# A three-block transformer kernel: other waits at the start and in its norms, masks on POOL, MLP features half by half

## The reference, cut to what matters

```python
for layer in range(2):
    hn = rmsnorm(h, mix_norm[layer])
    h = h + (moba_nsa_mixer(hn, ...) if layer % 2 == 0 else fox_mixer(hn, ...))
    h = h + sqrelu_mlp(rmsnorm(h, mlp_norm[layer]), mlp_w1[layer], mlp_w2[layer])
x = rmsnorm(h, final_norm)
# second_block: shifts, scales and gates sh1 ... gt3 come from silu(c) @ w_ada + b_ada
n = modulate(rmsnorm_2(x, g_ffn1), sh1, sc1); h = x + 0.5 * gt1 * swiglu(n, ...)
n = modulate(rmsnorm_2(h, g_mix), sh2, sc2);  h = h + gt2 * hybrid_mixer(n, ...)
n = modulate(rmsnorm_2(h, g_ffn2), sh3, sc3); h = h + 0.5 * gt3 * swiglu(n, ...)
return rmsnorm_2(h, g_final)
# in fox_mixer: s = q k / 8 + cum[query] - cum[key], masked where key > query, then softmax
```

## Time and profile before

| | us |
|---|---|
| median of 3 runs | 1121.64 |
| lowest and highest | 1120.15, 1125.65 |
| the profiled execution, its own time | 1123.69 |
| its span, first to last instruction | 1121.9 |
| PE busy in the span | 1086.5 (97%) |
| DVE busy | 783.7 (70%) |
| ACT busy | 648.2 (58%) |
| POOL busy | 98.6 (9%) |

### The profile page before, as it was taken

The page is one execution under the profiler, slowest core; times in us unless marked ns, Lnnn a source line. Parts: engine busy times, 40 slices in busy tenths (PEclk is TensorE's granted clock), DMA queues, the critical chain, the costliest instruction groups (busy, mean ns, idle before and its releaser), DMA issues.

```text
span 1121.9 us, 15908 instructions
## 1 busy us (share of the span) xinstructions
PE 1086.5 (97%) x6118; PEld 922.1 (82%) x6118; DVE 783.7 (70%) x1275; ACT 648.2 (58%) x1048; POOL 98.6 (9%) x195
## 2 busy tenths in 40 slices
PE   6999999999999999999999999999989999999997
PEld 5888878888887997888888778888878978888885
DVE  6567767777777666776766768887875766665565
ACT  6656766555566776664645664444455767444443
POOL 1022210010000121100000001101000110000000
PEclk9999999999999999999999999999999999999999
DMA  7742248888855633677778547777644434555551
GB/s 301 289 155 83 102 141 308 292 292 297 295 201 183 246 130 114 235 268 248 266 259 313 193 143 289 264 295 288 220 153 150 152 117 154 190 190 187 189 190 60
DMA packets 39515, 236.71 MB, mean 211 GB/s; under 512 B 4453, under 2 KB 4613, under 8 KB 16528
## 3 DMA queue, kind: packets, MB, share of 16 engines
q1 hardware_dynamic: 26640, 188.76, 46.9%
q0 software_dynamic: 12512, 46.26, 11.6%
q10 hardware_dynamic: 288, 0.68, 0.2%
HBM read 234.58 MB, written 1.10 MB: 210 GB/s over the span
## 4 chain that ended last, share of the span: by engine, by line
PE 84%; DVE 7%; ACT 5%; issue 2%; DMA 2%; SPq 0%; DVEq 0%; ACTq 0%
PE bank L1451 21%; PE bank L1420 15%; PE bank L1422 14%; PE bank L1421 14%; PE bank L1452 11%; PE bank L1625 2%; DMA raw<-in_stream 2%; DVE w_lo L981 1%; ACT w_hi L631 1%; PE bank L1607 1%; DVE w_lo L970 1%; PE bank L1596 1%; PE bank L1519 1%; ACT w_hi L620 1%; PE bank L1595 1%
## 5 line engine op out<-in xcount | busy, mean ns | idle before, releaser
L1451 PE MATMUL bank<-a_two,w_hi 128*128 128x512 f32 x1088 | 386.3, 398 | 0.0
L981 DVE TENSOR_TENSOR w_lo<-raw,w_hi 128x2048 fp32r<-128x2048 f32 x123 | 278.5, 2289 | 109.1 <-ACT w_hi L631 109.1
L1452 PE MATMUL bank<-a_two,w_lo 128*128 128x256 f32 x1088 | 305.2, 281 | 0.0
L631 ACT ACTIVATE w_hi<-raw 128x2048 fp32r<-128x2048 f32 x123 | 232.1, 1909 | 49.7 <-DMA raw<-in_stream 49.7
L1451 PEld LDWEIGHTS bank<-a_two,w_hi 128*128 128x128 f32 x1088 | 204.4, 188 | 49.6
L1452 PEld LDWEIGHTS bank<-a_two,w_lo 128*128 128x128 f32 x1088 | 205.4, 189 | 1.7
L1420 PE MATMUL bank<-w_lo,hid_hi 128*128 128x512 f32 x432 | 169.6, 393 | 3.6 <-DVE w_lo L981 2.4
L1421 PE MATMUL bank<-w_hi,hid_lo 128*128 128x512 f32 x432 | 168.5, 390 | 0.0
L1422 PE MATMUL bank<-w_hi,hid_hi 128*128 128x512 f32 x432 | 168.5, 390 | 0.0
L797 ACT ACTIVATE cross<-bank 128x256 f32<-128x256 f32 x136 | 44.8, 382 | 203.7 <-PE bank L1452 203.7
L970 DVE TENSOR_TENSOR w_lo<-raw,w_hi 128x1024 fp32r<-128x1024 f32 x102 | 124.5, 1238 | 31.3 <-ACT w_hi L620 30.5
(11 more groups left out here) (212 smaller groups left out, 1489.2 us busy)
## 6 DMA issues: line engine op xcount, KB each, us to landing
raw<-in_stream SPq DMA_DIRECT2D x173, 1024.0 KB, 5.0
ada_raw<-in_ada POOLq DMA_DIRECT2D x72, 512.0 KB, 5.2
cmpw<-in_stream SPq DMA_DIRECT2D x4, 1024.0 KB, 8.4
rel_band<-rel_scratch POOLq DMA_DIRECT2D x2, 1024.0 KB, 10.9
cum_row<-cum_scratch POOLq DMA_DIRECT2D x4, 512.0 KB, 7.2
h<-in_x SPq DMA_DIRECT2D x2, 512.0 KB, 6.5
raw<-in_stream SPq DMA_DIRECT2D x2, 512.0 KB, 7.6
silu_row<-in_c_row POOLq DMA_DIRECT2D x2, 512.0 KB, 4.6
```

Source lines behind the costliest of these rows:

```text
L631: nc.scalar.activation(w_hi[:, u % RING, :], raw[:, u % RING, :], ACT.Copy).then_inc(hi_ready, 2)
L981: nc.vector.tensor_tensor(w_lo[:, u % RING, :], raw[:, u % RING, :], w_hi[:, u % RING, :].bitcast(F32), ALU.subtract).then_inc(lo_ready, 2)
L1451: nc.tensor.matmul(ps[bank][:, 0:2 * T], wh[:, k, cols_], a_two[:, :, k, :], start=k == 0, stop=False)
L1452: ins = nc.tensor.matmul(ps[bank][:, T:2 * T], wl[:, k, cols_], a_hi[:, k, :], start=False, stop=k == KT - 1)
```

## The change

**Start.** DVE zeroes part of `probT` first, and PE runs `WARM` = 30 products on these zeros. PE no longer waits for `rpick` before it turns tile 0; tile 1 is turned after two value parts instead of three, and parts of unit 0 come before unit 1. ACT and DVE take the turned chunks one at a time (`split_no` numbers them), with the weights' halves between; two chunks share a bank (`turned_at`). The large second piece of `par` goes from ACT's queue, first of all, to SP's behind unit 3.

**First mixer.** `nq0` uses bank 7 instead of 4, so the wait for `pairs_taken` moves to `qm0`; `compress` of the second kind waits for bank 7; the turn of `hid30` moves from (`nq1`, 3) to (`qm0`, 0), and what hangs on it one tick later.

**Fox mixer.** The mask product on PE is gone. POOL adds the triangle to the key part of the bias, into `cum_early` (tile 0) and in place (tile 1).

**Norms.** The mean of the first half is taken while the second is squared, ACT's root adds the second sum as its bias, one Newton operation goes. ACT scales both tiles, in pieces of 256, 256 and 512 columns, and squares tile 1 between the chunks of tile 0. DVE makes the inverse root of tile 1 before the second weight half. `two_inverse_roots` is cut in `two_means`, `both_norms_root` and `first_norm_root`.

**MLPs.** Chunk 0 of a feature unit gets all eight contraction tiles, then chunk 1; `rests` takes chunk 0 when `half_done` says so. POOL begins the modulation's transfers only after the third unit of the MLP, `silu_row` is made after F3, and the columns begin with j = 3. **End.** The output goes out in quarters, half of them from ACT's queue.

The core of the diff:

```diff
+WARM = 30
+        cum_early = place("cum_early", [P, 16, P], at=V_at + 2 * D * 4)
         def fox_bias(hh, t):
-            return cum_row[:, hh, 0:(2 * P if t else P)]
+            return cum_row[:, hh, :] if t else cum_early[:, hh, :]
-        STACKS = {("kskw", 0): (5, True, 4), ("nq0", 0): (4, False, 4), ("nq1", 0): (5, False, 6),
+        STACKS = {("kskw", 0): (5, True, 4), ("nq0", 0): (7, False, 4), ("nq1", 0): (5, False, 6),
-            ... {"mlp0": (2, FF1 - 2), "mlp1": (2, FF1 - 4), "glu0": (1, FF2 - 3)}[name]
+            ... {"mlp0": (3, FF1 - 3), "mlp1": (3, FF1 - 5), "glu0": (1, FF2 - 3)}[name]
...
 # POOL
+            def mask(c):
+                pool.wait_ge(cum_landed[c], 16)
+                four = slice(4 * c, 4 * c + 4)
+                tri = pc_("tri", P).unsqueeze(1).to_broadcast([P, 4, P])
+                pool.tensor_tensor(cum_early[:, four, :], cum_row[:, four, 0:P], tri, ALU.add).then_inc(masked, 1)
+                pool.tensor_tensor(cum_row[:, four, P:T], cum_row[:, four, P:T], tri, ALU.add).then_inc(masked, 1)
+            pool.wait_ge(unit_used, FIRST["mlp0"] + 3)
             silu_input()
             modulation_weights(*ADA_OF["mlp0"])
...
 # ACT
             def root(name, t):
                 act.wait_ge(mean_ready, 2 * NORMS.index(name) + t + 1)
                 if name != "gf1":
-                    nc.scalar.activation(stat[:, 3, t:t + 1], stat[:, 2, t:t + 1], ACT.Sqrt).then_inc(root_ready, 1)
+                    act.wait_ge(sumsq, squares_before(name, t) + 2)
+                    nc.scalar.activation(stat[:, 3, t:t + 1], stat[:, 1, t:t + 1], ACT.Sqrt, bias=stat[:, 2, t:t + 1]).then_inc(root_ready, 1)
+            def scale(name, t):
+                act.wait_ge(inv_ready, NORM[name] + t + 1)
+                inv = fin[:, t, 12:13] if name == "gf1" else stat[:, 7, t:t + 1]
+                for c0, c1 in ((0, 256), (256, 512), (512, 1024)):
+                    nc.scalar.activation(tok[:, t, c0:c1], h[:, t, c0:c1], ACT.Copy, scale=inv).then_inc(rows_scaled_act, 1)
             def norm_turn(name, gain, shift=None):
-                for t in range(TT):
-                    squares(name, t)
-                    ...
+                squares(name, 0)
+                round_half()
+                scale(name, 0)
+                turned(name, 0, gain, shift, (0, 1))
+                square_half(name, 1, 0)
+                turned(name, 0, gain, shift, (2, 3))
+                square_half(name, 1, 1)
+                round_half()
+                root(name, 1)
+                scale(name, 1)
+                turned(name, 1, gain, shift)
             def mlp(name):
                 begin(name)
-                silu_of_c(1 if name == "mlp0" else 2)
...
+                        rests(0, MLP_BANKS[j % 2], crossed, HALF_BEFORE[name] + j - 1, u0 + n + 1)
+                        if j == 3:
+                            silu_of_c(1 if name == "mlp0" else 2)
...
 # DVE
             def norm_turn(name, sums, gain, shift=None, gate=None):
...
-                rest_half()
                 if fused:
                     weigh(1, 0)
+                    two_means(1)
                     weigh(1, 1)
-                    two_inverse_roots(1)
+                    both_norms_root(1)
                 else:
                     inverse_root(name, 1)
-                scale(name, 1)
+                rest_half()
                 turned(name, 1, gain, shift)
...
 # PE
             def wide_unit(u, banks):
-                for half in range(2):
-                    for nt in range(2):
-                        wide_part(u, banks[nt], nt, (half,))
+                for nt in range(2):
+                    wide_part(u, banks[nt], nt)
-                if kind == "fox":
-                    ins = nc.tensor.matmul(bank[:, P:3 * P], ident_r[:, :], tri_r[:, :].unsqueeze(1).to_broadcast([P, 2, P]),
-                                           start=False, stop=True)
+            for _n in range(WARM):
+                nc.tensor.matmul(ps[0][:, 0:P], probT[:, 0, 0:P], probT[:, 0, 0:P], start=True, stop=True)
-                    if tag == "nq0" and part == 0:
+                    if tag == "qm0" and part == 0:
                         pe.wait_ge(pairs_taken, 2)
```

More of the change, by code:

```diff
@@ L480, in build @@
         CROSS_BEFORE = {"mlp0": -4, "mlp1": 2 * FF1 - 8, "glu0": 4 * FF1 - 10, "glu1": 4 * FF1 + 2 * FF2 - 12}
+        HALF_BEFORE = {"mlp0": 0, "mlp1": FF1 - 2, "glu0": 2 * FF1 - 4, "glu1": 2 * FF1 + 2 * FF2 - 6}
         BEGIN = {"mlp0": 0, "mlp1": 1, "glu0": 2, "glu1": 3}
@@ L493, in ada_pieces @@
                 return range(0)
-            (first, last), j0, n = ADA_OF[name], *{"mlp0": (2, FF1 - 2), "mlp1": (2, FF1 - 4), "glu0": (1, FF2 - 3)}[name]
+            (first, last), j0, n = ADA_OF[name], *{"mlp0": (3, FF1 - 3), "mlp1": (3, FF1 - 5), "glu0": (1, FF2 - 3)}[name]
+            if j < j0:
+                return range(0)
             return range(first + (last - first) * min(j - j0, n) // n, first + (last - first) * min(j - j0 + 1, n) // n)
@@ L873, in even_extras @@
                         nc.scalar.activation(hid_e[:, v, :], ps[(2, 7)[v]][HD:HD + 30, 0:256], ACT.Copy).then_inc(hidden_half, 1)
-                for v, where in enumerate((("qm0", 0, 0), ("km0", 0, 2))):
+                for v, where in enumerate((("qm0", 0, 1), ("km0", 0, 2))):
                     if tick.at(*where):
@@ L950, in _ @@
                 act.wait_ge(inv_ready, NORM["last"] + t + 1)
-                nc.scalar.activation(tok[:, t, 0:512], ada_raw[:, t, 0:512], ACT.Copy, scale=stat[:, 7, t:t + 1]).then_inc(out_ready_act, 1)
+                for k in range(2):
+                    quarter = slice(256 * k, 256 * k + 256)
+                    nc.scalar.activation(tok[:, t, quarter], ada_raw[:, t, quarter], ACT.Copy, scale=stat[:, 7, t:t + 1]).then_inc(out_ready_act, 1)
+                for k in range(2):
+                    quarter = slice(256 * k, 256 * k + 256)
+                    act.wait_ge(out_ready_act, 2 * t + k + 1)
+                    act.dma_start(out[t * P:(t + 1) * P, quarter], tok[:, t, quarter]).then_inc(out_stored, 16)
         @block.vector
@@ new lines, in polish, with both_norms_root @@
+            def polish(t, v, root, y, b):
+                f = fin[:, t, :]
+                chain(nc.vector.reciprocal(f[:, y:y + 1], f[:, root:root + 1]))
+                chain(nc.vector.scalar_tensor_tensor(out=f[:, b:b + 1], in0=f[:, v:v + 1], scalar=f[:, y:y + 1], in1=f[:, y:y + 1],
+                                                     op0=ALU.mult, op1=ALU.mult))
+            def both_norms_root(t):
+                f = fin[:, t, :]
+                dve.wait_ge(mean_ready, NORM["gf1"] + t + 1)
@@ L1309, in even_extras @@
                                                 e, ALU.mult).then_inc(hidc_ready, 1)
[L1310 removed]
+                if tick.at("qm0", 0, 3):
                     dve.wait_ge(kc_hi, 1)
@@ L1403, in scale_out @@
             def scale_out(t):
-                half = slice(512, D)
-                nc.vector.scalar_tensor_tensor(out=tok[:, t, half], in0=h[:, t, half], scalar=stat[:, 7, t:t + 1], in1=row[:, half],
-                                               op0=ALU.mult, op1=ALU.mult).then_inc(out_ready, 1)
+                for k in range(2):
+                    quarter = slice(512 + 256 * k, 768 + 256 * k)
+                    nc.vector.scalar_tensor_tensor(out=tok[:, t, quarter], in0=h[:, t, quarter], scalar=stat[:, 7, t:t + 1], in1=row[:, quarter],
+                                                   op0=ALU.mult, op1=ALU.mult).then_inc(out_ready, 1)
             for t in range(TT):
@@ L1447, in wide_part @@
                 cols_ = slice(nt * P, nt * P + P)
-                for half in halves:
+                for half in range(2):
                     wait_weights(u, half)
@@ L1704, in even_extras @@
                         compress(c // 2, c % 2)
-                for v, where in enumerate((("nq1", 0, 3), ("km0", 0, 1))):
+                for v, where in enumerate((("qm0", 0, 0), ("km0", 0, 1))):
                     if tick.at(*where):
```

259 lines of the change are left out of this document (150 added, 109 removed).

## The result

The changed kernel takes 1112.37 us (median of 7 runs, 1111.13 to 1115.68) against 1120.87 us (7 runs, 1119.64 to 1125.65): a ratio of 0.9921, 95% interval 0.9910 to 0.9932, some 8.5 us faster. The time lies inside the predicted range, 4.6 us above the predicted value. Its profiled execution took 1113.3 us for a span of 1111.5, so the two profiled spans differ by 10.4 us.

What follows compares the result with a forecast made beforehand. The prediction took PE, busy nearly the whole span, as the bound. Its terms, -8.0 (start and first mixer), -0.7, -1.7, -2.35, -0.6 and -0.5, sum to -13.85, taking 1121.64 to 1107.8 us; range 1101.5 to 1114.5.

Steps and rivals of the forecast that it cites:

- masks of 2 us and more: Fox mixer: sign of a wrong prediction, which took POOL's masks at 1.2 us each.
- feature units of `glu0` that wait for weights: MLPs: sign of a wrong prediction, which took 0 for the weights of all 68 feature units.
- Start, -3.8 taken: Start: first value product 1.2 and 0.4 us earlier, 2.6 from the clock, less 0.4 for waits.
- The clock's 2.6 us: Start: 5.5 us of value products at the low level would run at the high one, about 2.6 us less.
- 30 take 4 us at the high level and twice that, 8, at the low: Start: the thirty products on zeros would be hidden, or late by a few tenths of a us.
- Rival A: Start: the clock is low when the values begin, taking back 2.6 us, 1110.4; chance 0.16.
- First mixer, -4.2 taken: First mixer: the pairs' wait goes, 1.8 us, the low clock behind it, 1.5, and the `hid30` wait, 0.9.
- `nq0` no longer waits for the pairs: -1.8: First mixer: the wait, moved to `qm0`, goes because ACT takes the pairs long before; 1.8 us.
- Rival B: First mixer: transfers bound it, half of start and mixer's gain, 4 us, is lost, 1111.8; chance 0.14.
- Fox, -0.7 taken: Fox mixer: sixteen mask products saved on PE, -2.7 us, against a new wait for POOL taken as 2.0.
- Rival C: Fox mixer: POOL's masks run slowly beside DVE, adding 9.5 us or more, 1117.3 to 1118.8; chance 0.09.
- Norms, -2.35 taken: Norms: shorter waits for scaled tiles, 0.85 us in `gf1`, 1.2 in `gmix` and `gf2`, 0.1 each in three others.

Runs made afterwards that it cites:

- e2: The changed kernel with 20 products on zeros instead of 30; 1115.12 us, ratio 0.9948.
- e3: The changed kernel with the wait for the pairs put back ahead of `nq0`; 1112.63 us, ratio 0.9928.
- e12: The changed kernel with the pairs' wait back ahead of `nq0` and unit 4 loaded only when unit 1 is used up; 1115.53 us, ratio 0.9943.
- e6: The changed kernel with `silu_row` and POOL's modulation transfers back at the beginning of `mlp0` and `mlp1`; 1115.89 us, ratio 0.9948.
- e7: The changed kernel with only POOL's modulation transfers begun at once in `mlp0` and `mlp1`, `silu_row` still after F3; 1113.40 us, ratio 0.9926.
- e10: The changed kernel with the old order in the feature units, half then chunk; 1114.97 us, ratio 0.9937.
- e4: The changed kernel with POOL's masks of pieces 2 and 3 behind the first and third head's scaling; 1112.37 us, ratio 0.9923.
- e11: The changed kernel with twenty products on zeros, masks of pieces 2 and 3 behind scalings, and the first norm's root one feature unit ahead; 1110.44 us, ratio 0.9894.
- e1: The changed kernel without the thirty products on zeros; 1114.86 us, ratio 0.9948.
- e8: The changed kernel with DVE's second weight half ahead of tile 1's inverse root in all norms but the first; 1128.08 us, ratio 1.0056.
- e5: The changed kernel with the first norm's inverse root one feature unit ahead of the final norm in `glu0`; 1113.73 us, ratio 0.9925.

## Why the prediction was right, and where not

The sum was -13.85; the traces give -10.4, the medians -8.5. The range held, and the mechanism in most stages; but the gains at the start, in fox, in `gmix` and `gf2` and in `glu0` came out smaller than forecast, and in the first mixer the size came without the cause named, which is luck. Two of the prediction's own signs of being wrong were seen: masks of 2 us and more, and feature units of `glu0` that wait for weights. Neither cost enough to leave the range.

- **Start, -3.8 taken, -2.0 measured.** The clock's 2.6 us was right in size. Mis-sized was the step "30 take 4 us at the high level and twice that, 8, at the low", hence "hidden": the price was read from turns of the same shape, at 0.14 each; a product leaves two records, which start 0.21 us apart at the low level and 0.11 at the high, so thirty would take some 13 or 7 us (an estimate from these distances) and with the rise between took 8.8, ending 1.9 us after the tile was there (e2). The wait for a chunk, for which 0.4 was taken off, was 1.0 at 17.19, and 0.1 for `w_lo` and 0.3 for a scaled tile stood before it. Rival A did not occur: in e2 and in the changed kernel eight turns stand between the products and the values, and the values start at the high level.
- **First mixer, -4.2 taken, -3.5 measured.** The size was near; the step "`nq0` no longer waits for the pairs: -1.8" named a cause that was not needed: e3 and e12 show that the earlier transfer is enough, and that the moved wait would be, no run shows. Rival B's limit is real: e2 gives back 1.2 of 1.9 us there. The wait of 0.9 for `hid30` is gone, but over `nq1` and `qm0`, where its turn now stands, PE gains 0.44.
- **Fox, -0.7 taken, 0.0 measured.** The wait came out near (2.2 us against 2.0), partly by luck: masks were both shorter and longer than assumed, and pieces 2 and 3 landed 4.7 and 6.3 us after their issue, not 7.2. The products saved were 2.3 us rather than 2.7. Rival C's cause is there, to a part of its price; e2 shows 4.6 us with the clock lower behind it.
- **`silu`, -1.7 taken, -2.1 measured.** Right by e6 and e7.
- **Norms, -2.35 taken, about -2.0 measured.** `gf1` gave more, `gmix` and `gf2` less (0.2 for 1.2): in `gmix` the root's result is there half a us earlier, counted from the end of `glu0`, and ACT's scaling, 1.5 us for the tile instead of DVE's 0.9, takes it back.
- **`glu0`, nothing taken, +1.25 measured.** This is the step that the prediction left out: of the two roots of `gf1` one did not go, it moved to `glu0`, and the lead of `w_lo` there was not looked at: DVE's chain is longer by the root's 0.83 us, and PE waits 0.67 and 0.44.
- **Ends, -0.6 and -0.5 taken, -0.95 and -0.35 measured**, the former not by the new order (e10). The end of `mlp1`, for which nothing was taken, gave 0.7 in the profile, by chance.

The 1.9 us by which the profiles differ more than the medians cannot be split among stages: there is one profile of before. That its waits were longer than usual is possible, and not shown.

## What to carry to other kernels

A step that vanishes in one place has to be found in the other: count its cost there, against the lead that the next engine has in that very unit. Where several edits fall on one wait, the one that ends it may be none that names it; ask which transfer the waiting engine was behind, and which buffer's release sent that out. And give a helper engine only what is needed next: with two of the masks behind scalings PE did not wait in e4 and e11.

## What was not expected of the hardware

Products at the start that are 0.43 us apart stand in windows whose granted clock reads 1.00; there only the starts tell. The window of e1, columns as above:

```profile
12.00:14.00 2.00, 2.00 (x7) 1.71 (x7) 1.64 (x6) 1.72 (x3) 0.64 (x1) 1.00 1.02 422
```

Pauses of like length ended differently. The granted clock fell to its lower level, for some microseconds, in or up to 1.5 us behind waits of 1.8 us (before; e8 in `gf2`), 2.0 (e8 and e10 in fox), 2.1 (e4 at 622), 2.3 (e12 at 46), 3.2 (e8 in `gf1`) and 4.6 (e2 in fox). It stayed at 1.00 behind 1.8 (e3 and e5 at the end of `mlp1`), 1.9 (e8 in `gmix`), 2.2 (the changed kernel in fox), 2.4 (e1 in fox) and 2.5 (before, in `gf1`): the length of the pause alone does not tell. In e4 and e12 it fell once, in `km0`, where PE waited for nothing longer than 0.1 us, at a cost of 1.2 us each; the other twelve traces keep 1.00 there. e4:

```profile
82.00:84.00 2.00, 2.00 (x15) 2.00 (x15) 0.30 (x2) 0.89 (x1) 0.83 (x2) 0.72 0.00 0
84.00:86.00 2.00, 2.00 (x11) 1.64 (x12) 0.88 (x5) 0.22 (x1) 0.00 (x0) 0.50 0.00 0
```

A full-precision product of 128 columns costs PE 0.43 us at the low level and 0.22 at the high one (the distances at the start), a turn 0.24 (e1) and 0.13.
